# Attention scores without a mask: a constant table starts each row's running product at its first visible key

## What is computed

```python
z = jnp.einsum('bqhd,bkhd->bhqk', qi, kj) * scale
causal = s_pos < t_pos
log_beta = jax.nn.log_sigmoid(z)
log_rem = jnp.where(causal, jax.nn.log_sigmoid(-z), 0.0)
suffix = lax.cumsum(log_rem, axis=3, reverse=True) - log_rem
weights = jnp.where(causal, jnp.exp(log_beta + suffix), 0.0)
o = jnp.einsum('bhqk,bkhd->bqhd', weights, vj)
```

## Time and profile before

| what | value |
|---|---|
| median of 3 runs | 1499.15 us (1498.51 to 1499.58) |
| profiled execution, its own time | 1496.84 us |
| span of that execution | 1495.1 us |
| PE busy | 1155.3 us, 77% |
| DVE busy | 508.1 us, 34% |
| ACT busy | 374.4 us, 25% |
| POOL busy | 26.5 us, 2% |

### The profile page before, as it was taken

The page is one execution under the profiler, slowest core; times in us unless marked ns, Lnnn a source line. Parts: engine busy times, 40 slices in busy tenths (PEclk is TensorE's granted clock), DMA queues, the critical chain, the costliest instruction groups (busy, mean ns, idle before and its releaser), DMA issues.

```text
span 1495.1 us, 19785 instructions
## 1 busy us (share of the span) xinstructions
PE 1155.3 (77%) x8185; PEld 686.2 (46%) x8185; DVE 508.1 (34%) x950; ACT 374.4 (25%) x618; POOL 26.5 (2%) x65
## 2 busy tenths in 40 slices
PE   8999899865666667556666666666665999999998
PEld 8777787421212212112122122121221788999887
DVE  6998876211101011011011010110110578676546
ACT  6658564201001001001000000000100364465434
POOL 1000220000000000000000000000000000000000
PEclk9999999988787777787778788787778999999999
DMA  8654526999999999999999999999999764455551
GB/s 303 197 200 139 210 87 261 395 427 427 427 427 426 427 429 427 427 429 427 428 427 427 428 428 427 428 428 426 429 427 428 265 211 142 169 185 182 195 177 50
DMA packets 58616, 493.31 MB, mean 330 GB/s; under 512 B 6666, under 2 KB 8260, under 8 KB 33988
## 3 DMA queue, kind: packets, MB, share of 16 engines
q1 hardware_dynamic: 57620, 491.54, 80.8%
q10 hardware_dynamic: 944, 1.05, 0.2%
HBM read 491.52 MB, written 1.05 MB: 329 GB/s over the span
## 4 chain that ended last, share of the span: by engine, by line
DMA 54%; PE 37%; DVE 7%; ACT 1%; issue 1%; SPq 0%; DVEq 0%; ACTq 0%
DMA arena<-in_expert_w_down 15%; DMA arena<-in_expert_w_up 12%; DMA arena<-in_expert_w_gate 12%; PE ps L1839 11%; PE ps L1930 7%; PE ps L1844 6%; DMA ring<-in_expert_w_gate 5%; DMA ring<-in_expert_w_down 5%; DMA ring<-in_expert_w_up 4%; PE ps L2286 4%; PE ps L2304 2%; DVE w_split L1125 2%; PE ps L1909 1%; PE ps L2100 1%; PE ps L2131 1%
## 5 line engine op out<-in xcount | busy, mean ns | idle before, releaser
L1125 DVE TENSOR_TENSOR w_split<-ring,w_split 128x1024 fp32r<-128x1024 f32 (+3 forms) x178 | 200.6, 1135 | 102.7 <-ACT w_split L701 101.3
L2286 PE MATMUL ps<-ring,arena 128*32 128x512 f32 x1024 | 163.5, 781 | 90.5 <-DMA ring<-in_expert_w_up 64.0
L2286 PE MATMUL ps<-arena 128*32 128x512 f32 x1024 | 160.1, 766 | 87.9 <-DMA arena<-in_expert_w_up 59.8
L701 ACT ACTIVATE w_split<-ring 128x1024 fp32r<-128x1024 f32 (+3 forms) x178 | 175.4, 991 | 192.8 <-PE ps L1844 136.5
L1575 DVE TENSOR_TENSOR arena<-arena,ps 128x512 f32<-128x512 f32 x16 | 11.0, 687 | 495.2 <-PE ps L2286 495.2
L1582 DVE TENSOR_TENSOR xs<-ps,xs 128x512 f32<-128x512 f32 x64 | 39.8, 684 | 296.5 <-PE ps L2312 296.5
L2286 PEld LDWEIGHTS ps<-ring,arena 128*32 128x32 f32 x1024 | 33.1, 129 | 212.0 <-DMA ring<-in_expert_w_up 104.4
L2286 PEld LDWEIGHTS ps<-arena 128*32 128x32 f32 x1024 | 33.1, 129 | 209.0 <-DMA arena<-in_expert_w_up 97.1
L1930 PE MATMUL ps<-hT_hi,w_split 128*128 128x256 f32 x608 | 111.4, 284 | 0.2 <-DVE arena L1746 0.2
L2304 PE MATMUL ps<-ring,arena 128*32 128x256 f32 x928 | 78.7, 496 | 39.1 <-DMA ring<-in_expert_w_down 36.8
L2304 PE MATMUL ps<-arena 128*32 128x256 f32 x1056 | 81.2, 459 | 35.5 <-DMA arena<-in_expert_w_down 31.8
(11 more groups left out here) (354 smaller groups left out, 1367.0 us busy)
## 6 DMA issues: line engine op xcount, KB each, us to landing
arena<-in_expert_w_gate SPq DMA_DIRECT2D x35, 2048.0 KB, 35.7
ring<-in_expert_w_up SPq DMA_DIRECT2D x35, 2048.0 KB, 35.9
ring<-in_expert_w_gate SPq DMA_DIRECT2D x29, 2048.0 KB, 36.1
arena<-in_expert_w_up SPq DMA_DIRECT2D x29, 2048.0 KB, 37.2
arena<-in_expert_w_down SPq DMA_DIRECT2D x25, 2048.0 KB, 34.3
ring<-in_expert_w_down SPq DMA_DIRECT2D x21, 2048.0 KB, 34.0
ring<-in_w_ff SPq DMA_DIRECT2D x32, 1024.0 KB, 5.0
ring<-in_w_in SPq DMA_DIRECT2D x24, 1024.0 KB, 5.1
```

What stands on the lines that cost most here:

```text
L701: act.activation(w_split[:, n % WBUFS, 0, 0:cols], slot_view(slot, cols)[:, n % 2, :], ACT.Copy).then_inc(split_hi, 1)
L1125: dve.tensor_tensor(buf[:, 1, :], w, buf[:, 0, :].bitcast(F32), ALU.subtract).then_inc(split_lo, 1)
L2286: m = pe.matmul(ps[j * CAP:(j + 1) * CAP, bank, :], xe[:, kt, :], w[:, r, j * FCOL:(j + 1) * FCOL], start=kt == 0, stop=kt == KT - 1, skip ...
```

## The change

No mask is added to the scores any more. `never`, `ident_r` and the four GpSimd instructions that built them are gone. Instead `whole_stick` has its 1 in another column in each row: row r of a block of queries has it at column 128 - r, which is the first visible key in the reversed order. Before that column the scan stays at 0, because `left` still has its 0 at the block's first column and nothing is added; so the weights of the invisible keys are 0 whatever their scores. Row 0 of the first block sees no key and has no 1; row 0 of the second block has it at column 128 of that block, for which the second select is one column longer.

```diff
-        never = sb("never", [P, P], F32R)
-        ident_r = sb("ident_r", [P, P], F32R)
...
-        N_MASKS = 5
+        N_MASKS = 4
...
-        raw_mask = hid[:, 0:P]
...
-            step(pool.memset(raw_mask, 0.0))
-            step(pool.affine_select(out=raw_mask, in_=raw_mask, compare_op=ALU.is_gt, fill=-2.0 ** 126, base=1 - P,
-                                    pattern=[[1, P]], channel_multiplier=1))
-            step(pool.tensor_scalar(never[:, :], raw_mask, 1.0, None, ALU.mult))
-            pool.tensor_scalar(ident_r[:, :], ident[:, :], 1.0, None, ALU.mult).then_inc(masks_ready, 1)
...
             step(pool.memset(whole_stick, 0.0))
-            step(pool.memset(segment_starts(whole_stick), 1.0))
+            whole = whole_stick.rearrange("p (m c) -> p m c", m=2)
+            for first in (whole[:, :, 0:P], whole[:, :, P:2 * P + 1]):
+                step(pool.affine_select(out=first, in_=first, compare_op=ALU.not_equal, fill=1.0, base=-P,
+                                        pattern=[[0, 2], [1, first.shape[2]]], channel_multiplier=1))
...
-                        pe.matmul(ps[:, 4 + m, at_col:at_col + width], qkT2[r, p, t0:t0 + P], qkT2[r, p, 2 * T - width:2 * T], start=True, stop=False)
-                    for m in range(2):
-                        last = pe.matmul(ps[:, 4 + m, at_col:at_col + P], ident_r[:, :], never[:, :], start=False, stop=True)
+                        last = pe.matmul(ps[:, 4 + m, at_col:at_col + width], qkT2[r, p, t0:t0 + P], qkT2[r, p, 2 * T - width:2 * T],
+                                         start=True, stop=True)
```

## The result

| | before | after |
|---|---|---|
| median of 22 runs, us | 1498.04 (1496.93 to 1501.68) | 1501.53 (1500.11 to 1504.71) |
| ratio of the times, 95% interval | | 1.0023 (1.0017 to 1.003) |
| profiled execution, us | 1496.84, span 1495.1 | 1502.63, span 1500.9 |

The change costs 3.5 us in the medians, with an interval of 2.5 to 4.5 us. The lowest of the 22 runs are 1496.93 and 1500.11, 3.2 apart. The forecast was 1499.1, "no change", and the highest end of its range 1500.3. Ahead of it stood a rival of 0.04 with 1502.4: that the new waits cost TensorE its clock.

A forecast was written before the change was run, and what follows sets the result against it. VectorE was taken to bound the second block's attention; gains of 0.0 at the gating matmuls and on GpSimd left 1496.8 us profiled, 1499.1 as median. Range 1498.4 to 1499.9, 8 in 10 from 1497.4 to 1500.3.

The forecast's parts named there:

- the new waits cost TensorE its clock: Second block's attention, 1230 to 1251.5: new gaps halve TensorE's clock for 3.3 us of work, 1502.4 us; chance 0.04.
- What bounds the stretch: Second block's attention: VectorE, not TensorE, sets when the gating matmuls start, through conv_read at 1251.33.
- The crack of 0.12 us: Before the gating matmuls: VectorE's signalling instruction ends at 1251.33, 0.12 us before their weight load at 1251.45.
- The work that is removed: TensorE in the attention: 16 mask matmuls, 0.65 us a pair, 2.60 us in all, 2.96 as upper end.
- The waits, their places and sizes: TensorE waits before pair 0's transposes, pair 3's transposes and the gating matmuls: about 0.65, 1.05 and 0.9 us.
- GpSimd's selects: Behind the experts: two selects replace a memset, 1.2 to 4.3 us, covered, cost nothing; VectorE not slowed.
- Granted clock 1.00 throughout: Expected sign in the changed kernel's trace: TensorE's granted clock stays at 1.00 despite the new waits.
- Here it would be busier than that: Against the clock loss: TensorE in the attention busier than around the routing wait, busy 3.47 of 5 us.
- the row of 1.05 us: Routing stage: TensorE waits 1.05 us for VectorE at granted clock 1.00, cited against a clock loss.
- The sum: Whole kernel: gain 0.0 at the gating matmuls and 0.0 from GpSimd, so 1496.8 us profiled, median 1499.1.

The follow-up runs named there:

- Experiments 4 and 5: Changed kernel with identity matmuls filling only the wait before pair 3's transposes (1497.32 us, ratio 0.9995), or only the one before the gating matmuls (1497.19 us, 0.9996).

## Why the prediction was wrong, by its steps

**What bounds the stretch: right, and shown.** VectorE sets when the gating matmuls start. They stand 25.02 us behind its first conv low part with the mask matmuls and without; moving 2.2 us of its own work behind them moves them to 22.77. The crack of 0.12 us between VectorE's end and a weight load was the right thing to read against a window that said 25.00 of 25.00 busy.

**The work that is removed: too small a term, without effect.** I priced it by starts, 0.65 us a pair and 2.60 in all, at most 2.96. A pair's scores take 1227.34 - 1226.49 = 0.85 us now. Before, the mask's two groups alone seemed to take 0.37 and 0.28, but the whole took from the start of the first score group to the next conv matmul at 1225.56, and that group is this row of the kernel before:

```profile
1223.86 0.49 PE L2363 MATMUL ps<-arena 64*128 64x128 f32 x4
```

That is 1.70 us, so 0.85 a pair and 3.4 in all: with nothing between them, the four score matmuls (eight records) also run closer together, which the distance from one mask group to the next one could not show. Here it only made the waits longer.

**The waits, their places and sizes: right.** Expected were about 0.65, 1.05 and 0.9 us; measured 0.91, 1.21 and 0.95. The first two are longer because more work had gone than I counted. Pair 3's transposes come 0.94 us earlier against VectorE than before (23.20 behind the first low part instead of 24.14), where the working had 0.90.

**GpSimd's selects: right.** They ran from 1177.41, took 1.81 us for both (between the 1.2 and 4.3 expected), and VectorE was not held. Of the kernel after, the selects, and a split subtraction of VectorE that ran beside them in 1.22 us, the mean of before:

```profile
1177.41 1.81 POOL L678 TENSOR_SCALAR_AFFINE_SELECT arena<-arena 128x256 f32<-128x256 f32 x2 [0.15 <-POOL arena L675]
1177.16 1.22 DVE L1120 TENSOR_TENSOR w_split<-ring,w_split 128x1024 fp32r<-128x1024 f32 x1
```

**"Granted clock 1.00 throughout": wrong, and this is the step that failed.** The prediction had the mechanism as a rival, "The new waits cost TensorE its clock", with a price that came out near: 3.3 us of work at half clock and 1502.4 us, against 3.1 us in the trace and a median of 1501.53. How long the clock would stay down, no row ahead of the result showed; 3.3 was an assumption, and that it came so close is luck. What was right is that each us of such work takes one more. The prediction gave the rival 0.04 because the routing stage has a wait of 1.05 us at a granted clock of 1.00. That row was read alone, and compared with each new gap alone, as if three gaps could be judged one by one. Experiments 4 and 5 show that each alone is indeed harmless. But between the two last ones there is only 0.88 us of transposes, and over both together TensorE is busy 1.05 of 3.20 us. The emptiest stretch of that length around the routing wait is this window of the kernel before:

```profile
261.20:264.40 3.20, 1.67 (x15) 1.42 (x13) 2.47 (x12) 1.89 (x4) 0.00 (x0) 1.00 0.99 425
```

1.67 of 3.20 us, and four of these matmuls (eight records) are ones that the kernel puts there to keep the clock. "Here it would be busier than that" was said of 5 us and of the first wait; for the last two it was false, and the forecast's own numbers could have shown it: 1.05 and 0.9 us of waiting with 0.57 us of transposes between them, some 0.6 busy of 2.5 us.

That would have raised the chance of the rival; it would not have settled it. The kernel before has far emptier stretches among its experts, and they do not all end alike. Two waits of TensorE for weights, equally long and before matmuls of the same line, then windows over the first wait, behind it, and behind the second:

```profile
324.00 1.92 PE L2286 MATMUL ps<-ring,arena 128*32 128x512 f32 x16 [2.97 <-DMA ring<-in_expert_w_up]
363.57 3.28 PE L2286 MATMUL ps<-ring,arena 128*32 128x512 f32 x16 [2.97 <-DMA ring<-in_expert_w_gate]
```

```profile
321.00:324.20 3.20, 0.23 (x8) 0.16 (x8) 0.00 (x0) 0.00 (x0) 0.00 (x0) 1.00 1.04 440
324.00:329.00 5.00, 2.69 (x23) 1.02 (x24) 0.69 (x1) 0.60 (x1) 0.00 (x0) 1.00 1.02 436
364.00:367.00 3.00, 2.85 (x16) 0.44 (x8) 0.00 (x0) 0.11 (x1) 0.00 (x0) 0.50 1.00 426
```

Behind the first the clock is 1.00 for the next five us, with TensorE busy 0.23 of 3.20 us in it; behind the second it is 0.50. So how empty a stretch is does not alone decide, and one row of a wait that did no harm says little of the next wait.

The Trainium skill, "TensorE: Matmul & The Clock Gate", section "Why this matters for your kernels", warns of idle gaps between bursts of matmuls. It speaks of single gaps longer than either of these two, so the row of 1.05 us, which the prediction set against it, did not speak against it. By its letter neither gap here should matter; here the measurement decides: gaps of 1.21 and 0.95 us in a row cost the clock, where single ones of 1.05 and 1.26 us did not.

**The sum.** In its place stands: gain at the gating matmuls 0.0, clock 3.1 us behind them. The remaining 0.4 of the 3.5 us of the medians is less than the runs can tell.

What stays open: why the clock falls behind these two waits in every run, as far as the times tell, and behind the longer ones among the experts only at times. Nothing between the two waits as they were and one of them filled was tried. And the first wait, 0.91 us before pair 0's transposes, with no second one near it, was never taken away alone: the clock is 1.00 from 1230 to 1250 in the kernel after, so it costs nothing that shows.

## What to carry to other kernels

When two engines are full in the same stretch, work taken from one of them becomes waits for the other; ask first which of them the next common point waits for, in tenths of a microsecond, by start times and not by busy shares. Then look at new waits that lie near one another together, since TensorE's clock may be lost by two of which neither costs it alone, and do not take one harmless wait elsewhere as a proof. To turn the saving into time, move the other engine's own less urgent work behind what is being waited for, and look at who is next to wait for it; if that can't be done, small matmuls in one of the waits can hold the loss at nothing, as they did here.

## What the hardware showed beyond that

The granted clock was still 1.00 in both waits; it fell once they were over, and was low from about 1255 to 1261, while TensorE was busy without a break: 3.1 us lost to a stretch of 3.2 us that itself delayed nothing. In the first block a single wait of 3.33 us is followed by a dip whose depth over the same 5 us was anything from 0.52 to 0.85 in ten executions of as many kernels; with the wait filled it was 1.00 in both that had it so. The runs with it filled lie lower (ratio 0.9989) and somewhat closer together, so part of the run-to-run spread of this kernel comes from there. And a wait of 2.97 us among the experts left the clock at 1.00 once and was followed by 0.50 another time in the same execution.
